# Where the next pair's projections stand in TensorE's order: key halves among the levels, three products at each place among the blocks

## The chip, the cores and the metric

The kernel runs on one core of one Trainium2 chip, in float32. The metric is the device time of one execution, in microseconds (us); the number before is the median of 3 runs.

## What is computed

The reference is one step of a two-layer decoder (RWKV-7 time mixing, then a Conformer convolution, each followed by an expert retrieval over 16384 experts). Only the time mixing is touched here. For each of the 1024 features the normed input is mixed with its neighbour token, and products with weights give receptance r, key k, value v; low-rank products give the decay w and the rate a:

```python
xm = x[None] + xx[None] * mu[:, None, None, :]
r, k, v = jnp.einsum('ibtd,ide->ibte', xm[:3], w_rkv)
w = -jax.nn.softplus(-(w0 + jnp.tanh(xw @ w1) @ w2).astype(f32)) - 0.5
a = jax.nn.sigmoid((a0 + (xa @ a1) @ a2).astype(f32))
kk = kk / jnp.maximum(jnp.sqrt(jnp.sum(kk * kk, axis=-1, keepdims=True)), 1e-12)
def step(S, inp):
    sa = jnp.einsum('bhij,bhj->bhi', S, -kk_t)
    S = (S * w_t[:, :, None, :] + sa[..., None] * (kk_t * a_t)[:, :, None, :]
         + v_t[..., None] * k_t[:, :, None, :])
    return S, jnp.einsum('bhij,bhj->bhi', S, r_t)
```

There are 512 prompt tokens and 8 x 8 sample tokens (576 columns in all), and 16 heads of 64 features.

## The kernel before

Two heads (128 features, one partition each) are a pair; there are 8 pairs, worked on one after the other by the function `wkv`. Each engine has its own hand-written instruction stream in `wkv` (blocks `pe`, `act`, `dve`, `pool`, `sp`), and engines wait for one another by counting semaphores. The class `Steps` gives each named step of an engine its count; the list of names (lines 256 to 272) must be in the order of the stream, and a name with "+" belongs to the next pair.

The scan over 512 prompt tokens is done in 4 blocks of 128. For pair i TensorE (lines 475 to 626) does, in this order:

- **bonus** (line 487) and the **grams** (lines 453 and 506): products between the factors at, bt, kt, rt of the pair, which VectorE makes last (`make_factors`, lines 838 to 848; its last instruction is the small MEMSET of line 848, and the first gram waits for it).
- **the levels** (lines 510 to 554), l = 1 to 6, which invert a triangular matrix by doubling. A level is: transposes and products "y" (lines 520, 528, 531) for two groups, a copy out of PSUM by ScalarE (line 722), a transpose to tokens in levels 1 to 3 (line 460), a place for filler, the products "dXT" (line 551), and an addition by VectorE (line 903, in the last level the copy of line 905), for which the next level's y waits.
- **the blocks** (lines 590 to 613), b = 0 to 3, a chain through the state: `rows_R` (lines 560, 563), ScalarE's copy (line 730), `rows_U` (line 572), ScalarE's copy (line 734), `rows_Y_S` (lines 577 to 585), VectorE's `update_state` (lines 913 to 920), and the next R waits for that. Between any two there is a place for filler.
- **mean** (line 617), what is left of the filler, the gate product (line 445) and **var** (line 625). VectorE centres y between mean and var (line 941), ScalarE squares it (line 772).

The filler is the generator `front(n)` with n = i + 1: the next pair's projections. `fill(count)` takes count steps of it. A step is one product of 128x128 weights with 288 columns (line 365; in the trace two matmuls, in the program's order one), or a pair of decay and rate products (lines 375, 376), or one norm sum (line 371). There are 52 steps: key half 0 (8), decay and rate (2), key half 1 (8), receptance half 0 and 1 (16), norm sums (2), value half 0 and 1 (16). By `fill` 8 are spent in the levels (0, 1, 1, 2, 2, 2), 40 among the blocks, and 4 are left behind mean. In the last pair (i = 7) there is no next front: its levels have no filler, and the blocks are filled with products of the output projection (line 469).

What VectorE does for the next pair stands in its stream between the block updates (lines 923 to 945): `logs` behind update 0, `rated_key` behind 1, `norm_floor` and two of four reciprocals behind 2, and behind update 3 the other two reciprocals, `unit_key`, `bonus_terms`, the centring of this pair's y, and `make_factors`. The core of it:

```python
update_state(3)
reciprocal(nrm, 2); reciprocal(nrm, 3)
unit_key(n)
bonus_terms(n)
dve.wait_ge(pe_s.sem, pe_s.value(f"mean.{i}"))
stt(out=in_two(yc[i]), ...)
make_factors(n)
```

ScalarE copies and squares the key (`key`, lines 643 to 650), makes the decay and rate (640, 641), the receptance (657), the key norm (661), the exponentials (674 to 679). SyncE's queue reloads the three weight buffers when k1, r1 and v1 of the pair are done (lines 335 to 340). Behind the eight pairs comes the retrieval and the convolution (lines 1000 and following), where 1152 indirect loads move most of the bytes.

Of the kernel before, what the change touches and what calls it, by code (L numbers as in the profile page):

```python
# [35 lines left out]
LEVELS = 7  # L36
# [150 lines left out]
def wkv(nc, K, I, normed, low_in, xm, y_out, hid_wa, hid_g, R, xm_at, wo_done, x_back, low2, prm, low_loaded, prm_loaded, wl):  # L187
# [8 lines left out]
    f = lambda: R.cut(N)  # L196
# [31 lines left out]
    yc, ysq = ([one] * (C - 1) + [Z.cut(T)] for one in (Q3.cut(T), Q3.cut(T)))  # L228
    sd = ysq
# [16 lines left out]
    def passes(front, steps):  # L246

        names = [f"{x}.0" for x in front.split()]
        for i in range(C):
            for x in steps:  # L250
                n = i + x.startswith("+") - x.startswith("-")
                if 0 <= n < C:
# [3 lines left out]
    pe_s = Steps(K.sem("wkv_pe"), passes("wa0 wa1 n1 n0 g",  # L256
                 ["bonus"] + [f"gram_{x}{e}" for x in ("L", "LT", "G", "RB", "RK") for e in range(2)]
                 + [x for l in range(1, LEVELS) for x in (f"y{l}_0", f"y{l}_1",
                                                         {1: "tok_v", 2: "tok_b", 3: "tok_k", LEVELS - 1: "+k0"}.get(l),
                                                         f"dXT{l}_0", f"dXT{l}_1") if x]  # L260
                 + "R0 +wa0 +wa1 U0 Y0 S0 R1 +k1 U1 Y1 S1 +r0 R2 U2 Y2 S2 +r1 +n1 +n0 R3 U3 +v0 Y3 S3 mean +v1 +g var".split()))
    act_s = Steps(K.sem("wkv_act"), passes("k0 k1 w0 a0 w1 a1 r0 r1 n1 n0 exps v0 v1 g",
                  ["gram_L0", "gram_L1"]
                  + [x for l in range(1, LEVELS) for x in (f"y{l}_0", f"y{l}_1",
                                                          {1: "tok_v", 2: "tok_b", 3: "tok_k"}.get(l)) if x]
                  + "+k0 R0 +w0 +a0 +w1 +a1 U0 R1 U1 +k1 +exps +r0 R2 U2 +r1 +n1 +n0 R3 U3 +v0 Y +v1 ysq +g sd".split()))
    dve_s = Steps(K.sem("wkv_dve"), passes("logs kf kk rk factors",
                  ["bonus"] + [f"{x}{e}" for x in ("maskLT", "level0_") for e in range(2)]
                  + [f"gram{x}{e}" for x in ("G", "RB", "RK") for e in range(2)]
# [12 lines left out]
    K_BANK, R_BANK, N_BANK, V_BANK, WA_BANK = (2, 3), (2, 3), (5, 4), (6, 7), ((4, 5), (6, 7))  # L282
# [43 lines left out]
    with nc.Block() as block:  # L326
# [35 lines left out]
        def _(pe):  # L362
            def project(n, src, j, h, name, bank):
                for k in range(C):
                    last = pe.matmul(ps[:, bank, 0:HALF], K.w[j][:, k, :], src[:, k, of_half(h)], start=k == 0, stop=k == C - 1)  # L365
                    if k == C - 1:
                        last.then_inc(pe_s.at(f"{name}{h}.{n}"), 1)
                    yield
# [51 lines left out]
            def front(n):  # L420

                pe.wait_ge(wl[0], n * 16 + 16)
                pe.wait_ge(dve_s.sem, dve_s.value(f"gramRK0.{n - 1}"))
                yield from project(n, xm[1], 0, 0, "k", K_BANK[0])
                pe.wait_ge(low_loaded, n * 16 + 16)
                for h in range(2):
                    decay_and_rate(n, h)
                    yield
                yield from project(n, xm[1], 0, 1, "k", K_BANK[1])
                pe.wait_ge(wl[1], n * 16 + 16)  # L430
                pe.wait_ge(act_s.sem, act_s.value(f"k0.{n}"))
                yield from project(n, xm[0], 1, 0, "r", R_BANK[0])
                pe.wait_ge(act_s.sem, act_s.value(f"k1.{n}"))
                yield from project(n, xm[0], 1, 1, "r", R_BANK[1])
                for h in (1, 0):
                    norm_sums(n, h)
                    yield
                pe.wait_ge(wl[2], n * 16 + 16)
                for h in range(2):
                    yield from project(n, xm[2], 2, h, "v", V_BANK[h])  # L440
# [36 lines left out]
            for i in range(C):  # L477
                ahead = front(i + 1) if i < C - 1 else output_so_far()

                def fill(count):  # L480
                    for _ in range(count):
                        next(ahead, None)
# [27 lines left out]
                for l in range(1, LEVELS):  # L510
                    corner = l == LEVELS - 1
                    for g in range(2):
                        if l > 1:
                            pe.wait_ge(dve_s.sem, dve_s.value(f"XT{l - 1}_{g}.{i}"))
                        elif g == 0:
                            pe.wait_ge(dve_s.sem, dve_s.value(f"gramG1.{i}"))
                        for b in range(2):
                            for e in range(2):
                                for j in range(1 if corner else 2):
                                    last = pe.matmul(ps[of_head(j ^ e), 4 * g + e, b * HD:(b + 1) * HD], XTd[of_head(j), e, 2 * g + b, :],  # L520
                                                     K.ident2[of_head(j)], start=True, stop=True)
                        if not corner:
                            pe.wait_ge(pool_s.sem, pool_s.value(f"co{l}_{g}.{i}"))
                        for b in range(2):
                            for e in range(2):
                                for j in range(0 if corner else 2):
                                    out = ps[of_head(j ^ e), 4 * g + e, Y_AT + b * HD // 2:Y_AT + (b + 1) * HD // 2]
                                    last = pe.matmul(packed(out, l), co[l % 2][g][of_head(j), e, b, :], later(XTd[of_head(j), e, 2 * g + b, :], l),
                                                     start=True, stop=True)
                                if corner:  # L530
                                    last = pe.matmul(ps[of_head(e), 4 * g + 1 - e, Y_AT + b * HD:Y_AT + (b + 1) * HD], L_low[HD:P, e, 2 * g + b, :],
                                                     XTd[HD:P, e, 2 * g + b, :], start=True, stop=True)
                        last.then_inc(pe_s.at(f"y{l}_{g}.{i}"), 1)
                    if l == 1:
                        pe.wait_ge(dve_s.sem, dve_s.value(f"gramRB1.{i}"))
                        tokens(i, "tok_v", v_s, 6)
                    if l == 2:
                        pe.wait_ge(dve_s.sem, dve_s.value(f"gramRK1.{i}"))
                        tokens(i, "tok_b", bt, 7)
                    if l == 3:  # L540
                        pe.wait_ge(act_s.sem, act_s.value(f"tok_v.{i}"))
                        tokens(i, "tok_k", kt, 6)
                    if i < C - 1:
                        fill((0, 0, 1, 1, 2, 2, 2)[l])
                    for g in range(2):
                        pe.wait_ge(act_s.sem, act_s.value(f"y{l}_{g}.{i}"))
                        for b in range(2):
                            for e in range(2):
                                for j in range(1 if corner else 2):
                                    q, width = of_head(j ^ e), HD if corner else HD // 2  # L550
                                    last = pe.matmul(ps[of_head(j), 4 * g + e, D_AT + b * width:D_AT + (b + 1) * width],
                                                     XY[g][q, e, b * HD:(b + 1) * HD],
                                                     XY[g][q, 1 - e if corner else e, Y_AT + b * width:Y_AT + (b + 1) * width], start=True, stop=True)
                        last.then_inc(pe_s.at(f"dXT{l}_{g}.{i}"), 1)
# [37 lines left out]
                rows_U(0)  # L592
                fill(3)
                rows_Y_S(0)
                fill(2)
                rows_R(1)
                fill(3)
                rows_U(1)
                fill(3)
                rows_Y_S(1)  # L600
                fill(4)
                rows_R(2)
                fill(3)
                rows_U(2)
                fill(3)
                rows_Y_S(2)
                fill(4)
                rows_R(3)
                fill(4)
                rows_U(3)  # L610
                fill(4)
                rows_Y_S(3)
                fill(4)
                pe.wait_ge(act_s.sem, act_s.value(f"Y.{i}"))
                pe.wait_ge(dve_s.sem, dve_s.value(f"state{NB - 1}.{i}"))
                for h in range(2):
# [19 lines left out]
        def _(act):  # L636
# [6 lines left out]
            def key(n, h):  # L643
                if n:
                    act.wait_ge(pe_s.sem, pe_s.value(f"k{h}.{n}"))
                else:
                    act.wait_ge(mix_pe.sem, mix_pe.value("key"))
                got = ps[:, K_BANK[h] if n else 4 + h, 0:HALF]
                act.activation(k_s[:, of_half(h)], got, ACT.Copy)
                act.activation(sq[:, of_half(h)], got, ACT.Square, scale=prm[:, K_K:K_K + 1]).then_inc(act_s.at(f"k{h}.{n}"), 1)  # L650
# [61 lines left out]
            for i in range(C):  # L712
# [15 lines left out]
                def rows_R(b):  # L728
                    act.wait_ge(pe_s.sem, pe_s.value(f"R{b}.{i}"))
                    act.activation(r_tok, ps[:, 0, 0:P], ACT.Copy).then_inc(act_s.at(f"R{b}.{i}"), 1)  # L730
# [5 lines left out]
                if more:  # L736
                    act.wait_ge(prm_loaded, n * 16 + 16)
                    key(n, 0)
                rows_R(0)
                if more:  # L740
                    decay_and_rate(n, 0)
# [2 lines left out]
                rows_R(1)  # L744
                rows_U(1)
                if more:
                    key(n, 1)
                    for part in range(3):
                        exps(n, part)
                    receptance(n, 0)  # L750
# [1615 lines left out]
```

## Time and profile before

| | |
|---|---|
| median of 3 runs | 3720.38 us (3717.39 to 3723.23) |
| profiled execution, its own time | 3720.96 us |
| its span | 3719.2 us |
| PE / DVE / ACT / POOL busy | 2813.9 / 2674.9 / 1453.8 / 1433.9 us |
| the eight pairs | about 86 to 578 us of the span |
| weight products of line 365 (7 pairs) | 672 matmuls, 189.5 us |

A busy time counts executed instructions only. Matmuls overlap by their pipeline, so the time that one takes of the engine is the distance between two starts, not its own duration. A row's "idle before" is the time in which the engine had nothing to run, with the instruction of the other engine that ended it. The clock column is TensorE's granted clock as a share of 2.4 GHz; 0.50 is 1.2 GHz.

### The profile page before, as it was taken

The numbers are of one execution on the slowest core, as the hardware profiler recorded it, in microseconds if no ns is written. First come the engines' busy times: TensorE is split into PE (matmuls) and PEld (weight loads), VectorE is DVE, ScalarE is ACT, GpSimd is POOL, SyncE is SP. The second block draws the span as 40 slices with busy tenths as digits, with TensorE's granted clock in tenths as the row PEclk, the third lists the DMA queues.
The fourth block names the chain that finished last, engine by engine and source line by source line (L and its number), as shares of the span: only waits on it lengthen the run. The fifth ranks groups of instructions, "written<-read, shape, count | busy, mean of one in ns | idle before, by whom it ended". The sixth has DMA issues, their size and how long they took to land.

```text
span 3719.2 us, 56236 instructions
## 1 busy us (share of the span) xinstructions
PE 2813.9 (76%) x20324; PEld 1333.2 (36%) x20324; DVE 2674.9 (72%) x6281; ACT 1453.8 (39%) x4371; POOL 1433.9 (39%) x1305
## 2 busy tenths in 40 slices
PE   7999996777787578787787768887886666666655
PEld 4777774323332124343332223443331222222111
DVE  7454644888676677877877778998676777777775
ACT  3434432333343344444444334444443333333333
POOL 0111111444444444434444444334454444444442
PEclk9999997888897779988798779999896877887878
DMA  2010114999999999999999999999999999999997
GB/s 91 21 40 21 40 47 161 425 426 425 426 426 427 426 427 416 382 414 421 411 420 427 427 426 425 400 374 384 396 419 426 426 426 427 426 427 426 427 426 311
DMA packets 198279, 1312.95 MB, mean 353 GB/s; under 512 B 25968, under 2 KB 34288, under 8 KB 44272
## 3 DMA queue, kind: packets, MB, share of 16 engines
q0 software_dynamic: 165888, 1208.03, 77.6%
q1 hardware_dynamic: 32112, 101.33, 7.0%
q8 instruction: 159, 2.61, 0.3%
q14 instruction: 120, 0.98, 0.1%
HBM read 1303.42 MB, written 5.86 MB: 352 GB/s over the span
## 4 chain that ended last, share of the span: by engine, by line
DMA 34%; DVE 21%; PE 19%; ACT 4%; issue 3%; DVEq 2%; POOL 1%; ACTq 1%; SPq 0%; POOLq 0%
DMA arena<-in_uv,arena 34%; DVE arena L1922 10%; PE psum L1334 8%; PE psum L1296 4%; PE psum L1494 3%; PE psum L1524 2%; DVE arena L2111 2%; ACT wbuf L1665 1%; DVE arena L1850 1%; ACT arena L1660 1%; POOL arena L1276 1%; DVE arena L2085 1%; DVE arena L1847 1%; DVE arena L1854 1%; ACT arena L1656 1%
## 5 line engine op out<-in xcount | busy, mean ns | idle before, releaser
L1334 PE MATMUL psum<-arena,wbuf 64*64 64x512 f32 (+1 forms) x8704 | 1455.5, 739 | 803.4 <-ACT wbuf L1665 797.5
L1276 POOL DMA_INDIRECT arena<-in_uv,arena x1152 | 1359.4, 1180 | 1737.6 <-PE psum L1334 1559.4
L1922 DVE SCALAR_TENSOR_TENSOR arena<-arena 128x1024 f32<-128x1024 f32 x1152 | 1392.3, 1222 | 480.5 <-DMA arena<-in_uv,arena 453.1
L1334 PEld LDWEIGHTS psum<-arena,wbuf 64*64 64x64 f32 (+1 forms) x8704 | 335.1, 153 | 1674.4 <-ACT wbuf L1665 1304.2
L1656 ACT ACTIVATE arena<-arena 128x2 f32<-128x2 f32 x576 | 117.0, 203 | 1663.3 <-DVE arena L1922 1644.0
L1665 ACT ACTIVATE wbuf<-cst,arena 128x64 f32<-128x64 f32 x1152 | 338.2, 340 | 40.8 <-issue 1.4
L1296 PE MATMUL psum<-arena,wbuf 128*128 128x256 f32 (+1 forms) x1024 | 311.8, 453 | 9.7 <-DVE arena L1933 5.8
L1660 ACT ACTIVATE arena<-arena 128x1 f32<-128x1 f32 x1152 | 276.7, 287 | 41.8 <-issue 2.4
L1296 PEld LDWEIGHTS psum<-arena,wbuf 128*128 128x128 f32 x1024 | 202.8, 208 | 170.5 <-issue 129.2
L365 PE MATMUL psum<-arena,wbuf 128*128 128x288 f32 x672 | 189.5, 414 | 0.0
L2111 DVE SCALAR_TENSOR_TENSOR arena<-arena,par 128x256 f32<-128x256 f32 x240 | 115.7, 482 | 48.3 <-ACT arena L1763 42.6
L1656 ACT ACT_TABLE_LOAD x107 | 137.3, 1283 | 19.3 <-DVE arena L1922 17.0
L1514 PE MATMUL psum<-arena 128*128 128x256 f32 (+1 forms) x512 | 137.0, 415 | 0.0
L962 POOL COPY arena<-arena 64x256 f32<-64x256 f32 x8 | 3.2, 397 | 331.6 <-DVE x L848 331.6
L365 PEld LDWEIGHTS psum<-arena,wbuf 128*128 128x128 f32 x672 | 117.9, 190 | 26.8 <-issue 2.7
L1494 PE MATMUL psum<-arena 128*128 128x320 f32 (+1 forms) x384 | 113.2, 439 | 16.7 <-ACT arena L1775 16.3
L1524 PE MATMUL psum<-arena 64*64 64x256 f32 x1024 | 123.3, 392 | 0.0
L1514 PEld LDWEIGHTS psum<-arena 128*128 128x128 f32 x512 | 93.6, 190 | 57.9 <-issue 36.8
L913 DVE SCALAR_TENSOR_TENSOR x<-psum,arena,cst 128x128 f32<-128x128 f32 x32 | 11.2, 350 | 138.4 <-PE psum L585 138.4
L1646 ACT ACT_TABLE_LOAD x79 | 101.4, 1283 | 4.9 <-issue 1.0
L1494 PEld LDWEIGHTS psum<-arena 128*128 128x128 f32 x384 | 72.0, 196 | 71.2 <-issue 34.7
L1922 DVE DVE_READ_ACCUMULATOR arena<-arena 128x1 f32 x1152 | 94.7, 82 | 0.0
(311 smaller groups left out, 3121.7 us busy)
## 6 DMA issues: line engine op xcount, KB each, us to landing
wbuf<-in_w_q SPq DMA_DIRECT2D x32, 1152.0 KB
arena<-in_uv,arena POOLq DMA_INDIRECT x1152
arena<-in_w_pw SPq DMA_DIRECT2D x16, 1024.0 KB
wbuf<-in_w_rkv SPq DMA_DIRECT2D x24, 512.0 KB, 4.4
arena<-in_w_o SPq DMA_DIRECT2D x16, 512.0 KB, 7.3
arena<-in_w_pw SPq DMA_DIRECT2D x16, 512.0 KB
x<-in_x SPq DMA_DIRECT2D x4, 576.0 KB, 7.3
arena<-in_state SPq DMA_DIRECT2D x8, 256.0 KB
```

Source lines behind the costliest of these rows:

```text
L365: last = pe.matmul(ps[:, bank, 0:HALF], K.w[j][:, k, :], src[:, k, of_half(h)], start=k == 0, stop=k == C - 1)
L1276: pool.indirect_dma_start(ring[:, g % RING, :], None, I["uv"][p // 2], bass.IndirectOffsetOnAxis(ap=idx[:, s % 4, j:j + 1], axis=0)).then_ ...
L1296: last = pe.matmul(ps[:, 7, 0:WIDTH[half]], K.w9[j][:, k, :], h[half][:, k, :], start=k == 0, stop=k == C - 1)
L1334: last = pe.matmul(ps[e * HD:(e + 1) * HD, 2 * (u % 2) + a if u < NB else 4, :], diag[t, g % DIAGS, :], ring[t, g % RING, D + e * 512:D + ...
L1494: last = pe.matmul(ps[:, BANK[c % 2], 0:WIDTH[half]], weights[c % 2][:, k, :], src[:, k, :], start=k == 0, stop=k == C - 1)
L1514: last = pe.matmul(out, wb[j][:, k, :], h[half][:, k, :], start=k == 0, stop=k == C - 1)
L1524: last = pe.matmul(part[q], tap_diags[q, k, :], ups[c % 2][q, k:k + 2 * P], start=k == 0, stop=k == PE_TAPS - 1)
L1656: act.activation(gelu[:, q], dots[:, q], ACT.Gelu)
L1660: act.activation(coef[:, c:c + 1], gelu[:, c:c + 1], ACT.Copy, scale=share[:, s % 4, j + k:j + k + 1])
L1665: act.activation(diag[:, (g + k) % DIAGS, :], K.ident2, ACT.Copy, scale=coef[:, c:c + 1]).then_inc(diag_ready, 1)
L1922: stt(out=row, in0=row, scalar=1.0, in1=tok[p % 2][:, UNITS[p % 2].index(u), :], op0=ALU.mult, op1=ALU.mult, accum_out=dots[:, g % COLS:g ...
L2111: last = stt(out=out, in0=up[:, k:k + 2 * P], scalar=K.par[:, TAP0 + k, c:c + 1], in1=out, op0=ALU.mult, op1=ALU.add)
```

## The change

The steps of `front` stand in another order: both key halves first, then decay and rate. The fills in levels 1 to 6 become 0, 2, 2, 4, 4, 4 (16 steps, before 8), and each of the 12 places from R0 to behind S3 takes 3 steps (36; before 40, of 2, 3 and 4), so that none is left behind mean. ScalarE takes key half 1 before its R0 copy, not behind U1, and TensorE waits for the rate of half 1 (`a1`) before the norm sums, which the wait for `k1` did before. The numbers of steps and the work are the same.

```diff
-                                                         {1: "tok_v", 2: "tok_b", 3: "tok_k", LEVELS - 1: "+k0"}.get(l),
+                                                         {1: "tok_v", 2: "tok_b", 3: "tok_k", LEVELS - 3: "+k0", LEVELS - 1: "+k1"}.get(l),
-                 + "R0 +wa0 +wa1 U0 Y0 S0 R1 +k1 U1 Y1 S1 +r0 R2 U2 Y2 S2 +r1 +n1 +n0 R3 U3 +v0 Y3 S3 mean +v1 +g var".split()))
+                 + "R0 +wa0 +wa1 U0 Y0 S0 R1 +r0 U1 Y1 S1 +r1 R2 +n1 +n0 U2 Y2 S2 R3 +v0 U3 Y3 S3 +v1 mean +g var".split()))
...
                 yield from project(n, xm[1], 0, 0, "k", K_BANK[0])
+                yield from project(n, xm[1], 0, 1, "k", K_BANK[1])
                 pe.wait_ge(low_loaded, n * 16 + 16)
                 for h in range(2):
                     decay_and_rate(n, h)
                     yield
-                yield from project(n, xm[1], 0, 1, "k", K_BANK[1])
...
                 yield from project(n, xm[0], 1, 1, "r", R_BANK[1])
+                pe.wait_ge(act_s.sem, act_s.value(f"a1.{n}"))
                 for h in (1, 0):
                     norm_sums(n, h)
...
-                        fill((0, 0, 1, 1, 2, 2, 2)[l])
+                        fill((0, 0, 2, 2, 4, 4, 4)[l])
...
                 rows_Y_S(0)
-                fill(2)
+                fill(3)
                 rows_R(1)
                 fill(3)
                 rows_U(1)
                 fill(3)
                 rows_Y_S(1)
-                fill(4)
+                fill(3)
                 rows_R(2)
                 fill(3)
                 rows_U(2)
                 fill(3)
                 rows_Y_S(2)
-                fill(4)
+                fill(3)
                 rows_R(3)
-                fill(4)
+                fill(3)
                 rows_U(3)
-                fill(4)
+                fill(3)
                 rows_Y_S(3)
-                fill(4)
+                fill(3)
...
                     key(n, 0)
+                    key(n, 1)
                 rows_R(0)
...
-                    key(n, 1)
                     for part in range(3):
                         exps(n, part)
```

How TensorE's order moves, at two places (line numbers behind line 425 are one higher in the changed kernel). The first is levels 4 and 5 of pair 0, before:

```order
L520 MATMUL psum<-cst,arena 64x64 x8
L528 MATMUL psum<-arena 64x32 x8
L365 MATMUL psum<-arena,wbuf 128x288 x2
L551 MATMUL psum<-arena 64x32 x16
L520 MATMUL psum<-cst,arena 64x64 x8
L528 MATMUL psum<-arena 64x32 x8
L520 MATMUL psum<-cst,arena 64x64 x8
L528 MATMUL psum<-arena 64x32 x8
L365 MATMUL psum<-arena,wbuf 128x288 x2
L551 MATMUL psum<-arena 64x32 x16
```

and with the change:

```order
L521 MATMUL psum<-cst,arena 64x64 x8
L529 MATMUL psum<-arena 64x32 x8
L365 MATMUL psum<-arena,wbuf 128x288 x4
L552 MATMUL psum<-arena 64x32 x16
L521 MATMUL psum<-cst,arena 64x64 x8
L529 MATMUL psum<-arena 64x32 x8
L521 MATMUL psum<-cst,arena 64x64 x8
L529 MATMUL psum<-arena 64x32 x8
L365 MATMUL psum<-arena,wbuf 128x288 x4
L552 MATMUL psum<-arena 64x32 x16
```

Four weight products instead of two stand between y and dXT of each of these levels.

The second place is the seam from S3 of pair 0 (line 585) to the grams of pair 1, before:

```order
L585 MATMUL psum<-arena 128x128
L365 MATMUL psum<-arena,wbuf 128x288 x4
L617 MATMUL psum<-x,cst 128x256 x2
L365 MATMUL psum<-arena,wbuf 128x288 x4
L445 MATMUL psum<-arena 128x288 x2
L625 MATMUL psum<-x,cst 128x256 x2
L487 MATMUL psum<-arena,cst 128x288 x2
L453 MATMUL psum<-arena 64x64 x40
```

and with the change:

```order
L586 MATMUL psum<-arena 128x128
L365 MATMUL psum<-arena,wbuf 128x288 x3
L618 MATMUL psum<-x,cst 128x256 x2
L446 MATMUL psum<-arena 128x288 x2
L626 MATMUL psum<-x,cst 128x256 x2
L488 MATMUL psum<-arena,cst 128x288 x2
L454 MATMUL psum<-arena 64x64 x40
```

One product ahead of mean and all four behind it have gone from here.

## Rows read from the trace of the kernel before

**Rows 1.** Windows: start:end, us, busy of each engine, clock, DMA share, GB/s.
```profile
207.90:268.60 60.70, 57.31 (x890) 45.70 (x890) 33.23 (x69) 24.98 (x52) 9.10 (x19) 1.00 0.09 32
```

**Rows 2.** VectorE's last instruction of make_factors: duration, first and last start.
```profile
L848 DVE MEMSET x<- x8: 165/165/165, 85.3 to 509.6; 128x128 f32 x8
```

**Rows 3.** Waits from 86 to 510 us: sum, times, longest.
```profile
DVE arena L827 <- ACT arena L661: 15.7, 7, 2.3
...
PE psum L453 <- DVE x L848: 7.0, 7, 1.0
...
PE psum L560 <- DVE arena L905: 4.9, 7, 0.7
...
PE psum L560 <- DVE x L920: 2.2, 7, 0.6
```

**Rows 4.** PE's timeline, level 4 of pair 2: start, us, what, [idle before].
```profile
222.15 1.24 PE L365 MATMUL psum<-arena,wbuf 128*128 128x288 f32 x4
223.32 0.67 PE L551 MATMUL psum<-arena 64*64 64x32 f32 x32
224.16 0.46 PE L520 MATMUL psum<-cst,arena 64*64 64x64 f32 x16 [0.18 <-DVE arena L903]
```

**Rows 5.** ACT's timeline: level 4's two copies, then the square before var.
```profile
221.80 0.96 ACT L722 ACTIVATE arena<-psum 128x384 f32<-128x384 f32 x2 [1.37 <-PE psum L528]
...
264.80 0.62 ACT L772 ACTIVATE x<-x 128x512 f32<-128x512 f32 x1
```

**Rows 6.** PE's timeline, filler before R1 and before R2 of pair 2.
```profile
236.38 1.14 PE L365 MATMUL psum<-arena,wbuf 128*128 128x288 f32 x4
238.14 0.49 PE L560 MATMUL psum<-x,arena 128*128 128x128 f32 x2 [0.62 <-DVE x L920]
...
243.72 2.11 PE L365 MATMUL psum<-arena,wbuf 128*128 128x288 f32 x8
245.67 0.38 PE L560 MATMUL psum<-x,arena 128*128 128x128 f32 x2
```

**Rows 7.** DVE's timeline: the last step of update 1.
```profile
244.78 0.29 DVE L920 TENSOR_SCALAR x<-arena 128x128 f32<-128x128 f32 x1
```

**Rows 8.** PE's timeline, the seam from S3 of pair 2 to pair 3.
```profile
259.32 0.39 PE L585 MATMUL psum<-arena 128*128 128x128 f32 x2
...
261.49 1.03 PE L617 MATMUL psum<-x,cst 128*128 128x256 f32 x4
262.35 2.11 PE L365 MATMUL psum<-arena,wbuf 128*128 128x288 f32 x8
264.30 1.14 PE L445 MATMUL psum<-arena 128*128 128x288 f32 x4
265.48 1.13 PE L625 MATMUL psum<-x,cst 128*128 128x256 f32 x4
266.44 1.14 PE L487 MATMUL psum<-arena,cst 128*128 128x288 f32 x4
268.59 0.58 PE L453 MATMUL psum<-arena 64*64 64x64 f32 x22 [1.01 <-DVE x L848]
```

**Rows 9.** DVE's timeline, the same seam.
```profile
259.75 0.35 DVE L913 SCALAR_TENSOR_TENSOR x<-psum,arena,cst 128x128 f32<-128x128 f32 x1 [2.46 <-PE psum L585]
...
260.44 1.96 DVE L823 RECIPROCAL arena<-arena 128x144 f32<-128x144 f32 x2
...
263.94 0.68 DVE L941 SCALAR_TENSOR_TENSOR x<-psum,x 128x512 f32<-128x512 f32 x1
...
268.37 0.17 DVE L848 MEMSET x<- 128x128 f32 x1
```

**Rows 10.** Windows, PE alone: start:end, us, PE busy, granted clock, DMA share, GB/s.
```profile
508.00:510.00 2.00, 1.00 (x12) 1.00 0.94 358
...
518.00:520.00 2.00, 0.70 (x32) 1.00 0.13 47
520.00:522.00 2.00, 1.82 (x64) 0.87 0.04 8
522.00:524.00 2.00, 2.00 (x48) 0.50 0.00 0
...
584.00:586.00 2.00, 0.28 (x2) 1.00 0.36 55
586.00:588.00 2.00, 0.00 (x0) 0.58 0.82 336
```

More of the change, by code:

```diff
@@ L265, in wkv @@
                                                           {1: "tok_v", 2: "tok_b", 3: "tok_k"}.get(l)) if x]
-                  + "+k0 R0 +w0 +a0 +w1 +a1 U0 R1 U1 +k1 +exps +r0 R2 U2 +r1 +n1 +n0 R3 U3 +v0 Y +v1 ysq +g sd".split()))
+                  + "+k0 +k1 R0 +w0 +a0 +w1 +a1 U0 R1 U1 +exps +r0 R2 U2 +r1 +n1 +n0 R3 U3 +v0 Y +v1 ysq +g sd".split()))
     dve_s = Steps(K.sem("wkv_dve"), passes("logs kf kk rk factors",
```

## The prediction

> **What bounds the kernel now.** I read the page first: over the whole span DMA and VectorE lead the chain that ended last, but that is the retrieval behind the pairs. It starts from the pairs' output, so what the pairs take is added to the end one for one, and only they are changed. Second, the windows: over one pair TensorE is busy 57.31 of 60.70 us, VectorE 33.23, ScalarE 24.98, at full clock [rows 1]. The eight factor memsets lie from 85.3 to 509.6 us, so a pair is (509.6 - 85.3) / 7 = 60.6 us [rows 2]. TensorE's stream is the bound, and its idle time is all that a new order of the same work can win. Third, the waits show where that is: 1.0 us a pair at the seam, for the factors; 0.7 us before R0; 0.3 us a pair before R1 (2.2 us over 7) [rows 3]; and 0.18 us at each of five levels [rows 4]. The other places where one engine hands to another are covered by filler.
>
> **The price of a product.** Before R2 eight matmuls, four products, start at 243.72 and R2 starts at 245.67 [rows 6]: 1.95 / 4 = 0.49 us each. The change moves such products and adds none.
>
> **1. Eight more products in the levels (+3.9 us a pair).** Filler there covers ScalarE's two copies out of PSUM. In level 4 they start at 221.80 and end 0.96 later, at 222.76 [rows 5]; the two products run from 222.15, and dXT starts at 223.32 [rows 4], 0.56 us after the second copy. So two products already cover the copies, and two more stand in the open. In levels 2 and 3 the tokens' transposes and one product stand there already. The level's own wait, 0.18 us before the next y [rows 4], lies behind dXT, where no filler stands, and stays; so does the 0.7 us before R0 [rows 3]. Sum: 8 x 0.49 = +3.9 us. Bounds: all eight in the open, +3.9; two or so hidden in unseen slack, +3.0. I take 3.9.
>
> **2. Four of them come out from among the blocks, ahead of S3 (-1.8 us a pair).** Before R1 there is one more product (2 to 3): it costs 0.49 and fills the 0.3 us of wait, so +0.2. Before R2 and R3 there is one less (4 to 3). Update 1 ends at 244.78 + 0.29 = 245.07 [rows 7], and three products from 243.72 end at 245.18 [rows 6]: three just cover the update, so each place gives its whole 0.49. If the update were late there as it is before R1, up to 0.3 of each would come back as a wait. The places behind R3 and U3 (4 to 3 each) must cover a ScalarE copy, which three products do behind R1, U1, R2 and U2 with no wait on TensorE in the list; 0.49 each. Sum: 0.2 - 4 x 0.49 = -1.8; bounds -2.0 and -1.2.
>
> **3. Five come out of the seam, behind S3 (0 us).** This is the step that decides. From S3 on VectorE works without a gap worth naming: update 3 at 259.75, reciprocals at 260.44, the centring at 263.94, the memset that frees the grams until 268.37 + 0.17 = 268.54, and the grams start at 268.59 [rows 8, 9]. That is 8.8 us of VectorE from S3, in an order that the change doesn't touch; TensorE's 4 + 4 products lie beside it. With one product less ahead of mean and none behind it, mean runs from about 261.0 (it was 261.49), and the centring at 263.94 is not waiting for it either way. The gate product follows and ends near 263.0. Var has to wait for ScalarE's square, 264.80 + 0.62 = 265.42 [rows 5], and starts at 265.48 as before; bonus follows at 266.44, the grams at 268.59 [rows 8]. So 5 x 0.49 = 2.4 us of work go, and a new wait of 2.4 us before var takes their place. What the earlier norm sums bring does not help here: the wait that they shorten (15.7 us over 7 pairs, VectorE on the key norm) [rows 3] lies before update 3, where VectorE then waits for S3 anyway, 2.46 us [rows 9]. Gain 0; bounds 0 and -0.2.
>
> **4. ScalarE and the queues (0).** Key half 1 (two activations of 0.4 to 0.5 us) now stands before the R0 copy. Key half 0 no longer arrives there late, R0 waits for VectorE's last copy in any case, and ScalarE has time between. If it were late, `U0` and all of the chain behind it would wait; I put at most +0.3 a pair. Weight reloads are released earlier or at the same time. The new wait for `a1` stands many us behind the rate. In the last pair the output products, smaller than 0.49 each, spread differently: 0, with -2 to +2.
>
> **5. The clock at the seam (+3 in all, bounds 0 and +14).** Today the seam leaves TensorE idle for 1.0 us and the clock stays at 2.4 GHz, as in the stretch 508 to 510 [rows 8, 10]. It does not after longer pauses: after 518 to 520 with 0.70 of 2 us busy it fell to 1.2 GHz, and after 584 to 586 with 0.28 busy too [rows 10]. The new seam holds 2.4 us idle, then 1.95 us of var and bonus, then 1.0 us idle: more idle than today's and less than behind 584, so I expect a fall at some of the seven seams. What one costs: var and bonus take 3.9 instead of 1.95 us and end at 269.4, 0.8 us behind the memset; a fall that comes later slows the first grams instead, some 2 us at most. Four seams at 0.8 make 3. The Trainium skill, "TensorE: Matmul & The Clock Gate", section "HAM oscillation — how this bites in real kernels", describes this: waits between bursts of matmuls bring the clock back to half. [...]
>
> **Sum.** Steps 1 to 4: 3.9 - 1.8 + 0 + 0 = +2.1 us a pair, x 7 pairs with a next front = +15; step 5: +3. The sum is made against the profiled execution, 3720.96 us (span 3719.2), which lies 0.6 over the median: 3739, against the median 3738. By the bounds of the steps: 7 x (3.0 - 2.0 - 0.2) = +6 and 7 x (3.9 - 1.2 + 0.3) + 14 = +35; neither end has all its parts at once, so the likeliest case's own range is 3730 to 3750.
>
> **The rivals.**
> *The clock stays low into the levels.* In pair 7, whose levels have no filler, the clock stays at 0.50 from 522 us on [rows 10]. If the seam's fall outlasts the grams (4.5 us at full clock, so +4) and level 1 (+2), a seam costs 6, and four seams 24: 15 + 24 = +39, 3759. Against it: the grams are dense work, and the levels hold more filler now, which speaks for a rise.
> *The levels hide the products (not slower).* If TensorE's time in levels 4 to 6 were set by the chain y, copy, dXT, addition, and not by its own stream, six of the eight products would be free: 7 x (3.9 - 2.9 - 1.8) = -6, 3715. It turns the sign from the point where five of eight are hidden. Against it is the 0.56 us between the copy's end and dXT [rows 4, 5], and that the only wait left stands behind dXT.
> *The seam was TensorE's and not VectorE's.* Were the memset pulled ahead by what TensorE sheds, 7 x 2.4 = 17 would come back: 15 - 17 = -2, 3719, no difference. For it speaks that TensorE waits only 1.0 us there; against it VectorE's unbroken rows [rows 9].
> *The change does nothing measurable,* because a slip elsewhere (a stalled fetch of instructions, a late reload) covers it: 3722.
>
> **How the numbers follow.** No change can be told within 0.2%, 7.4 us, that is 3713 to 3728. The forecast, 3738: 0.75. The clock low into the levels, 3759: 0.09. Levels hide the products: 0.05, a third of it faster by over 0.2%. The seam was TensorE's: 0.06. Nothing measurable: 0.05. So faster 0.02, same 0.13, slower 0.85. The range, 3727 to 3751, takes in the forecast's own range and a part of the cases on either side.
>
> **What would show it.** Right: line 365 unchanged in count (672 matmuls) and busy time; a level 4 that is 0.97 us longer; TensorE idle for about 2.4 us before var (line 626 then) with ScalarE's square as releaser, and still 1.0 before the grams; 8.8 us from S3 to the memset; the memsets 62.7 us apart; the key norm's wait of VectorE gone and its wait for S3 longer; stretches of clock below 1.00 at some seams. Wrong: pairs 60 to 61 us apart, or the memset less than 8.5 us behind S3 (step 3), or levels 4 to 6 of unchanged length (step 1), or new waits before R1 to R3 (step 2).

## The result, and the profile after

| | before | with the change |
|---|---|---|
| median of 7 runs each | 3722.53 us | 3733.18 us (3731.77 to 3734.87) |
| ratio, 95% interval | | 1.0033 (1.0023 to 1.0042) |
| profiled execution, its span | 3720.96, 3719.2 us | 3733.08, 3731.3 us |
| eight memsets of `make_factors`, start to start | 60.6 us | 62.9 us |

The changed kernel is slower by 10.65 us, 12.1 us between the two profiled executions; 3738 was forecast, within 3727 to 3751. The change's own line numbers are one higher behind line 425.

VectorE's last instruction of `make_factors` answers to [rows 2]; (526.7 - 86.4) / 7 = 62.9 us a pair:

```profile
L849 DVE MEMSET x<- x8: 165/165/165, 86.4 to 526.7; 128x128 f32 x8
```

The waits from 86 to 525 us (sum, times, longest) answer to [rows 3]:

```profile
PE psum L626 <- ACT x L773: 16.3, 7, 2.3
...
PE psum L561 <- DVE arena L906: 4.9, 7, 0.7
...
PE psum L454 <- DVE x L849: 3.8, 4, 1.1
```

The first is new: TensorE waits 2.3 us before var at all seven seams. The wait before R0 is as it was, the one before R1 (VectorE's line 921 now) has gone from TensorE's list.

TensorE's timeline of pair 2: level 4, then the filler before R2. It answers to [rows 4, 6].

```profile
228.88 2.21 PE L365 MATMUL psum<-arena,wbuf 128*128 128x288 f32 x8
231.02 0.67 PE L552 MATMUL psum<-arena 64*64 64x32 f32 x32
231.86 0.46 PE L521 MATMUL psum<-cst,arena 64*64 64x64 f32 x16 [0.18 <-DVE arena L904]
...
253.37 1.62 PE L365 MATMUL psum<-arena,wbuf 128*128 128x288 f32 x6
254.83 0.42 PE L561 MATMUL psum<-x,arena 128*128 128x128 f32 x2
```

The filler of level 4 takes 231.02 - 228.88 = 2.14 us instead of 1.17, so its two added products cost 0.97, and the level's own wait of 0.18 us is still there. Before R2 three products take 1.46 us (254.83 - 253.37) and R2 starts with no wait: they just cover the update.

The seam of pair 2 on TensorE, then on VectorE and ScalarE, answers to [rows 5, 8, 9]:

```profile
267.11 0.39 PE L586 MATMUL psum<-arena 128*128 128x128 f32 x2
267.33 1.62 PE L365 MATMUL psum<-arena,wbuf 128*128 128x288 f32 x6
268.79 1.02 PE L618 MATMUL psum<-x,cst 128*128 128x256 f32 x4
269.65 1.14 PE L446 MATMUL psum<-arena 128*128 128x288 f32 x4
273.13 1.57 PE L626 MATMUL psum<-x,cst 128*128 128x256 f32 x4 [2.33 <-ACT x L773]
274.50 2.13 PE L488 MATMUL psum<-arena,cst 128*128 128x288 f32 x4
276.55 1.85 PE L454 MATMUL psum<-arena 64*64 64x64 f32 x80
```

```profile
267.53 0.35 DVE L914 SCALAR_TENSOR_TENSOR x<-psum,arena,cst 128x128 f32<-128x128 f32 x1 [3.43 <-PE psum L586]
...
271.73 0.68 DVE L942 SCALAR_TENSOR_TENSOR x<-psum,x 128x512 f32<-128x512 f32 x1
...
276.15 0.17 DVE L849 MEMSET x<- 128x128 f32 x1
```

```profile
272.44 0.63 ACT L773 ACTIVATE x<-x 128x512 f32<-128x512 f32 x1 [3.04 <-DVE x L942]
```

From update 3 to the memset VectorE takes 276.15 - 267.53 = 8.62 us; before it took 268.37 - 259.75 = 8.62 us [rows 9]. TensorE has shed five products and stands still instead. At this seam bonus takes 2.05 us to the next start, not 1.07, since the clock fell. Granted clock (the last but two) in windows of 1 us there:

```profile
273.00:274.00 1.00, 0.87 (x3) 0.84 1.03 369
...
275.00:276.00 1.00, 1.00 (x4) 0.50 0.76 269
...
277.00:278.00 1.00, 1.00 (x66) 0.96 0.00 0
```

It fell like that at three of the seven seams.

Read off VectorE's starts (memset, and line 913, now 914, for S0 to S3), the typical pair is this; the first two columns are of the trace before and after, the others of experiments told below:

| us | before | change | before_levels8 | blocks_to_seam | after_tail4 |
|---|---|---|---|---|---|
| memset to S0 | 28.88 | 32.77 | 32.77 | 28.96 | 32.37 |
| S0 to S3 | 22.81 | 20.96 | 22.81 | 20.96 | 19.50 |
| S3 to memset | 8.62 | 8.62 | 8.62 | 8.62 | 8.62 |
| mean of 7 pairs | 60.6 | 62.9 | 64.5 | 59.0 | 60.8 |

The typical pair leaves out what pairs 0 to 2 have besides (0.4 to 1.3 us each, with and without the change); that stands in the means. The change has its three falls of the clock in pairs 1, 3 and 6 on top.

### The profile page after: what moved, and what is told of

It is laid out like the page before. It is cut to its first block, busy times and chain, and to the rows that moved or that the text cites. A ratio compares the mean times of both kernels' runs of the same rounds, so it can differ in the third digit from the quotient of the medians.

```text
span 3731.3 us, 56236 instructions
## 1 busy us (share of the span) xinstructions
PE 2802.5 (75%) x20324; PEld 1329.4 (36%) x20324; DVE 2674.1 (72%) x6281; ACT 1451.8 (39%) x4371; POOL 1428.0 (38%) x1305
## 4 chain that ended last, share of the span: by engine, by line
DMA 35%; DVE 21%; PE 18%; ACT 4%; issue 3%; DVEq 2%; POOL 1%; ACTq 1%; SPq 0%; POOLq 0%
DMA arena<-in_uv,arena 34%; DVE arena L1923 10%; PE psum L1335 8%; PE psum L1297 4%; PE psum L1495 3%; DVE arena L2112 2%; PE psum L1525 2%; ACT wbuf L1666 1%; POOL arena L1277 1%; ACT arena L1661 1%; DVE arena L1851 1%; DVE arena L2086 1%; DVE arena L1848 1%; DVE arena L1855 1%; ACT arena L1657 1%
## 5 line engine op out<-in xcount | busy, mean ns | idle before, releaser
L1515 PEld LDWEIGHTS psum<-arena 128*128 128x128 f32 x512 | 93.6, 190 | 58.1 <-issue 36.9
```

The lines of the kernel that those rows point to most:

```text
L1515: last = pe.matmul(out, wb[j][:, k, :], h[half][:, k, :], start=k == 0, stop=k == C - 1)
```

## The experiments

The theory: the seam from S3 to the memset is set by VectorE's 8.62 us, so products put there are free up to TensorE's wait, and every product elsewhere costs its 0.49 us. The rivals: TensorE's own work sets the seam too (every product costs the same anywhere); or the levels hide a part of their filler.

**after_seam4: four useless products in the new wait.** Their result is not used.

```diff
 gate_terms(i + 1)
+for k in range(4):
+    pe.matmul(ps[:, 2, 0:HALF], K.headones, hid_g[:, 0:HALF], start=True, stop=True)
```

> The changed kernel with four more products (the gate hidden values against a constant, 288 columns, result unused) behind the gate product of each of the seven pairs that have a next one, ahead of var. If VectorE's chain of 8.6 us from S3 to the factor memset sets the seam, they stand in the 2.3 us of wait before var: memsets stay 62.9 us apart, time 3733 us, 3731 to 3735, and the clock doesn't fall at the seams any more. If TensorE's own work sets it, each costs 0.49 us: 7 x 1.95 = 13.6 more, 3747 us.

Measured: 3733.51 us, ratio 1.0028 (1.0015 to 1.0040), where the change itself has 1.0033. The memsets lie 62.7 us apart. The seam of pair 2 on TensorE:

```profile
270.16 2.10 PE L625 MATMUL psum<-arena,cst 128*128 128x288 f32 x8
272.65 1.13 PE L628 MATMUL psum<-x,cst 128*128 128x256 f32 x4 [0.39 <-ACT x L775]
273.62 1.14 PE L488 MATMUL psum<-arena,cst 128*128 128x288 f32 x4
275.90 1.63 PE L454 MATMUL psum<-arena 64*64 64x64 f32 x80 [1.15 <-DVE x L851]
```

The wait before var is 0.39 instead of 2.33 us: 1.95 us of products went in and moved nothing. The clock doesn't fall at any seam here, and with that the pairs behind a fall are 0.4 to 0.6 us shorter: memset to S0 is 32.77 in pairs 3 and 6, where it was 33.17 and 33.20 with the change, and 34.04 instead of 34.63 in pair 1. 62.9 - 62.7 = 0.2 us a pair, 1.4 us in all, is the price of the falls by these two profiles; the medians are too rough for it.

**before_seam4: the same four in the kernel before.** The same edit behind `gate_terms(i + 1)`.

> The kernel before with the same four added products behind the gate product of each of seven pairs. If the seam is VectorE's chain with TensorE 1.0 us short of it, the first two are free and the others are in the open: 7 x (1.95 - 1.01) = 6.6 more than before, 3729 us. If every product on TensorE costs its 0.49 us: 13.6 more, 3736 us.

Measured: 3722.69 us, ratio 1.0005 (0.9996 to 1.0015). The memsets lie 61.1 us apart, 0.5 a pair more, where 0.94 was expected. The seam:

```profile
266.45 1.14 PE L445 MATMUL psum<-arena 128*128 128x288 f32 x4
267.43 2.10 PE L624 MATMUL psum<-arena,cst 128*128 128x288 f32 x8
269.37 1.02 PE L627 MATMUL psum<-x,cst 128*128 128x256 f32 x4
270.23 1.14 PE L487 MATMUL psum<-arena,cst 128*128 128x288 f32 x4
271.30 1.63 PE L453 MATMUL psum<-arena 64*64 64x64 f32 x80
```

Now TensorE goes through without a wait, and start-to-start distances give the true room. Gate to the next start is 0.98 us, var to bonus 0.86, bonus to grams 1.07. Before they were 1.18, 0.96 and 2.15 [rows 8]. So the seam had 0.20 + 0.10 + 1.08 = 1.38 us of room, not the 1.01 of the idle column: two short waits before var and bonus didn't show as idle time, since the modelled end of a matmul (0.40 us behind its start) overlapped them. 1.95 - 1.38 = 0.57, and memset to S0 grew from 28.88 to 29.43. The theory holds, its room was mis-sized, and with it the 3729 us that were expected.

**before_levels8: eight useless products in the levels.** Two behind the filler of each of levels 3 to 6; the result is not used.

```diff
 fill((0, 0, 1, 1, 2, 2, 2)[l])
+for k in range(2 if l > 2 else 0):
+    pe.matmul(ps[:, 3, 0:HALF], K.headones, hid_g[:, 0:HALF], start=True, stop=True)
```

> The kernel before with two added products (result unused) behind the filler of each of levels 3 to 6 of seven pairs. If filler there stands in the open: 7 x 8 x 0.49 = 27 more, 3750 us, and S0 comes 3.9 us later behind the memset. If the chain of y, copy, dXT and addition covers a part of it, as the rival said, less: 3736 us or under if half is covered.

Measured: 3749.39 us, ratio 1.0073 (1.0056 to 1.0090). In level 5 of pair 2 the two added ones and dXT behind them:

```profile
236.53 1.24 PE L365 MATMUL psum<-arena,wbuf 128*128 128x288 f32 x4
237.61 1.13 PE L546 MATMUL psum<-arena,cst 128*128 128x288 f32 x4
238.67 0.67 PE L553 MATMUL psum<-arena 64*64 64x32 f32 x32
```

Memset to S0 is 32.77, the same 3.89 us as with the change. The levels hide none of eight products; that rival is gone.

**after_tail4: one step of the change undone, with real work.** Two products instead of three behind each of R0 to R3, and four left behind mean again; the levels stay as changed.

```diff
 rows_R(0)
-fill(3)
+fill(2)
```

and the same behind `rows_R(1)`, `rows_R(2)` and `rows_R(3)`, with the names of TensorE's steps in the new order.

> The changed kernel with one product less at each of the four places behind R0 to R3 (2 instead of 3) and these four products left behind mean again, where the kernel before has them. The work is the same. If they stand for nothing at the seam (VectorE's chain), each of the four saves its 0.49 us among the blocks: S0 to S3 shorter by 1.5 (three of the places lie there), S3 to memset 8.62 as ever, memset to S0 32.8 less 0.5, memsets 60.9 us apart, 7 x 1.95 = 13.6 under the changed kernel: 3720 us, which is the kernel before within 2. If the seam is TensorE's, 3733 us as with the change; if two products behind R don't cover ScalarE's copy, between the two.

Measured: 3720.60 us, ratio 1.0001 (0.9992 to 1.0010), and 60.8 us a pair. The four products stand in the seam of pair 2:

```profile
262.87 2.10 PE L365 MATMUL psum<-arena,wbuf 128*128 128x288 f32 x8
264.81 1.14 PE L446 MATMUL psum<-arena 128*128 128x288 f32 x4
266.34 1.13 PE L626 MATMUL psum<-x,cst 128*128 128x256 f32 x4 [0.39 <-ACT x L773]
...
269.59 1.63 PE L454 MATMUL psum<-arena 64*64 64x64 f32 x80 [1.15 <-DVE x L849]
```

They are free there, and they save what they cost where they stood: S0 to S3 is 19.50 instead of 20.96 us, 1.46 for three, and memset to S0 0.40 less for the fourth. So the change's eight products in the levels (+3.9) are paid back, all but 0.2 us, by eight from the blocks (-1.85 ahead of S3 by the change, and 1.46 + 0.40 = 1.86 a pair more here). What the change lost, it lost by emptying the seam. Two products behind R cover ScalarE's copy nearly as well as three: what was saved there is within 0.1 us of the full 0.49 each.

**blocks_to_seam: the products from the blocks into the seam.** The levels as before, three products at each place, eight behind mean. For this the norm sums go ahead of receptance half 1, and ScalarE takes receptance half 1 behind U3, value half 0 behind Y. The first of these lines stands behind S0, the second behind S1, S2, R3, U3 and S3.

```diff
-fill(2)
+fill(3)
...
-fill(4)
+fill(3)
```

> The kernel before with the levels' filler as it was (8), three products at each of the twelve places among the blocks, and the eight that are left behind mean; the norm sums stand before receptance half 1, and ScalarE takes receptance half 1 behind U3 and value half 0 behind Y. The half of the change that takes products from the blocks, without the half that puts them into the levels. From S0 to S3 1.9 us less, at the seam TensorE's work grows by 3 products to 0.4 us over VectorE's chain: 7 x (0.4 - 1.9) = -10, 3712 us. If the seam had been TensorE's own: 7 x (3 x 0.49 - 1.9) = -3, 3720 us. If a copy of ScalarE comes late by its new order: slower than 3722.

Measured: 3711.11 us, ratio 0.9963 (0.9949 to 0.9978). The seam of pair 2:

```profile
258.37 1.02 PE L617 MATMUL psum<-x,cst 128*128 128x256 f32 x4
259.23 4.05 PE L365 MATMUL psum<-arena,wbuf 128*128 128x288 f32 x16
263.12 1.14 PE L445 MATMUL psum<-arena 128*128 128x288 f32 x4
264.09 1.03 PE L625 MATMUL psum<-x,cst 128*128 128x256 f32 x4
264.95 1.14 PE L487 MATMUL psum<-arena,cst 128*128 128x288 f32 x4
266.02 1.63 PE L453 MATMUL psum<-arena 64*64 64x64 f32 x80
```

TensorE has no wait left there. The three products more in the seam cost 0.08 us (memset to S0, 28.88 to 28.96), which is 3 x 0.49 less the room of 1.38 found by before_seam4. S0 to S3 is 1.85 us shorter, and a pair takes 59.0 us.

**hole_at_R0: one more hole.** As blocks_to_seam, with one of level 6's two products behind dXT, in the wait before R0.

```diff
-fill((0, 0, 1, 1, 2, 2, 2)[l])
+fill((0, 0, 1, 1, 2, 2, 1)[l])
...
+if i < C - 1:
+    fill(1)
 pe.wait_ge(dve_s.sem, dve_s.value(f"XT{LEVELS - 1}_1.{i}"))
```

> As blocks_to_seam, and one of level 6's two products stands behind dXT instead of ahead of it, in the 0.7 us in which TensorE waits for VectorE's copy before R0. If that wait is a hole: memset to S0 0.3 to 0.5 us less, 7 x 0.4 = 3 under blocks_to_seam, 3708 us. If the product delays R0 because ScalarE's key copy comes behind it, or dXT waits for ScalarE's copy: 3711 us or more.

Measured: 3710.08 us, ratio 0.9964 (0.9950 to 0.9977). The pairs are 0.4 us shorter, as expected: memset to S0 28.42 in the shortest, memsets (496.3 - 86.0) / 7 = 58.6 us apart. The whole is not measurably faster than blocks_to_seam: 3 us were expected, and the intervals are about 5 us to either side. The last pair took 36.90 us from memset to S0 in this profiled execution (30.59 in that one), more than the seven pairs won. What happens there was the next question.

**before_last8 and hole_and_last8: filler in the last pair's levels.** Eight useless products in levels 2 to 6 of pair 7 alone.

```diff
+else:
+    for k in range((0, 0, 1, 1, 2, 2, 2)[l]):
+        pe.matmul(ps[:, 3, 0:HALF], K.headones, hid_g[:, 0:HALF], start=True, stop=True)
```

> The kernel before with eight added products (result unused) in levels 2 to 6 of the last pair alone, as the other pairs have there. If the last pair's sparse levels are what lets the clock fall, it stays at 2.4 GHz there, and memset to S0 of pair 7 is 28.9 us like the others' instead of 32.4: 3.5 us less, 3718 us. If the fall and the 1.5 us stall come from something else (the load of the output weights), the products add up to 3.9: 3725 us.

> hole_at_R0 and before_last8 together. By the theory 3.0 to 3.5 us under hole_at_R0 if its last pair loses the clock as before, less if it falls late there as in the changed kernel (29.4): 3705 to 3708 us. By the rival 3709 to 3712.

Measured: 3721.14 us, ratio 0.9999 (0.9990 to 1.0008), and 3709.83 us, ratio 0.9968 (0.9958 to 0.9979); neither can be told from the kernel it was made from. In before_last8 the clock is low for 3.4 us instead of 17, and memset to S0 of pair 7 is 31.20 against 32.43 before, where 28.9 was expected. The 1.2 us are a balance: the clock and a pause shorter by 0.3 us give back more than the eight products cost (3.9 us at full clock); the runs don't part these. In hole_and_last8 it is 36.6. TensorE's waits from 495 to 534 us in that kernel:

```profile
PE psum L520 <- issue: 3.8, 2, 2.7
```

It stands still for 3.8 us with no semaphore that the profile shows to wait for, while the output weights' loads run or just behind them; in the kernel before it was 1.5 us, with the change 0.6 and 0.4. (The last section has what the traces say of these pauses.) Dense levels alone don't make the last pair short.

**before_paced, hole_paced, hole_paced_last8: the loads one by one.** The theory was that eight loads of 512 KB issued together hold up what TensorE waits for.

```diff
 for c in range(C):
+    if c >= 2:
+        sp.wait_ge(pe_s.sem, pe_s.value(("gram_L1", "y1_1", "y2_1", "y3_1", "y4_1", "y5_1")[c - 2] + f".{i}"))
     sp.dma_start(wo[:, c * C:(c + 1) * C, :], I["w_o"][c]).then_inc(wo_loaded, 16)
```

> The kernel before, where SyncE starts the third to eighth of the eight loads of the output weights (512 KB each) one by one, behind the last pair's gram L and behind y of levels 1 to 5, instead of all at once. If TensorE's 1.5 us pause in the last pair comes from these loads, it goes or shrinks under 0.5 us, memset to S0 of pair 7 falls from 32.4 to about 30, less if the clock falls later too: 1.5 to 4 us less, 3718 us. If the pause has another cause: as before, 3721 us.

> hole_at_R0 with the paced loads. Its last pair took 36.9 us from memset to S0, with 2.1 us of pause and 28 us of half clock. If the loads are the cause: 29 to 31 us there, 3703 us. If not: 3710 us.

> hole_and_last8 with the paced loads. It had 3.8 us of pause and 36.6 us from memset to S0 in the last pair. If the loads are the cause and the added products keep the clock: 28.5 us there, 3702 us. If not: 3710 us.

Measured: 3718.68 us, ratio 0.9995 (0.9986 to 1.0004); 3702.95 us, ratio 0.9954 (0.9940 to 0.9967); 3703.81 us, ratio 0.9960 (0.9946 to 0.9973). TensorE's waits of this kind in the last pair, for before_paced and then for hole_paced:

```profile
PE psum L533 <- issue: 1.3, 1, 1.3
...
PE psum L530 <- issue: 0.5, 1, 0.5
```

```profile
PE psum L553 <- issue: 1.3, 1, 1.3
```

So the pause isn't removed: 1.8 us against 1.5 in the kernel before, and 1.3 against 2.1 in hole_at_R0. Memset to S0 of the last pair is 30.61 and 30.12 us, as expected if the loads were the cause, but the pause that was to go is still there, and with the loads as they were this stretch took anything from 29.4 to 36.9 us. Only in hole_paced_last8 there is none, and there the last pair takes 28.74 us from memset to S0 at full clock (fields: us, busy of each engine, clock 1.00):

```profile
495.90:524.70 28.80, 26.98 (x724) 22.34 (x723) 15.43 (x35) 9.85 (x22) 9.13 (x18) 1.00 0.41 135
```

The theory on the loads is not shown by one such profile. The medians of the last two are the lowest of the study, 17 us under the kernel before and 30 under the changed one, but their intervals overlap those of hole_at_R0 and blocks_to_seam; that pacing the loads helps is not shown either.

## Why the prediction was right, and where its sizes were off

**Step 1, the levels: right.** +3.9 was forecast, memset to S0 grew from 28.88 to 32.77, +3.89, and before_levels8 gives the same 3.89 with other products.

**Step 2, the blocks: right.** -1.8 was forecast, S0 to S3 went from 22.81 to 20.96, -1.85. No new wait before R1 to R3, and three products cover the update as worked out.

**Step 3, the seam: right, and it decides.** VectorE's 8.62 us from S3 to the memset is the same in every kernel of the study, with from 3 to 12 products of filler beside it. The five products that left became the wait of 2.33 us before var (forecast 2.4). after_seam4 shows that four put back cost nothing, after_tail4 that leaving real ones there gives the whole loss back. The key norm came early, as said, and VectorE waits for S3 longer, 3.43 against 2.46 us. What was mis-sized is the room before the change: 1.38 us and not 1.01 (before_seam4). It doesn't enter the sum.

**Steps 1 to 3 together.** +2.04 a pair, 14.3 us over seven. The memsets' distance from first to last grew from 424.3 to 440.3, 16.0 us; the seams' clock and a scatter of 0.3 us are the rest.

**Step 5, the clock: mechanism right, size off.** Forecast four falls at 0.8 us, 3 in all, with a bound of 14. There were three at 0.4 to 0.6, 1.4 in all by after_seam4. A fall costs less than worked out because its first half lies in the room beside VectorE: at the seam shown bonus takes 1 us longer, of which 0.2 reach the grams. The rival with the clock low into the levels didn't come: the clock is back within 4 us, during the grams. The Trainium skill, "TensorE: Matmul & The Clock Gate", section "HAM oscillation — how this bites in real kernels", shows such falls behind waits of 3 to 5 us between bursts of matmuls. No wait of a seam is longer than 2.3 us here, so that example says nothing for a fall at every seam; the trace has one at three of seven.

**Step 4, the last pair: the term that failed.** It was put at 0, between -2 and +2. From its memset to the start of the last output products it took 578.29 - 509.63 = 68.66 us before and 592.36 - 526.74 = 65.62 with the change, -3.0. Ten profiled executions of kernels whose last pair has no filler in its levels, the two of before and change among them, have memset to S0 at 29.4 to 36.9 us, so the 3.0 is within what this pair does by itself: it all lies there, 32.43 against 29.42. What the change does to this pair is seen behind S0, and comes to nothing. S0 to S3 is 21.31 us in every kernel with the fills of before and 19.99 with three at each place, 1.32 less, and from S3 to the last output products (line 631, now 632) it is 14.92 and 16.21 us, 1.29 more: the output products only moved. Two windows from the memset to S0, before and with the change (the third from the end is the clock):

```profile
509.60:542.10 32.50, 29.17 (x706) 25.84 (x707) 15.55 (x36) 9.97 (x21) 9.19 (x18) 0.74 0.27 102
```

```profile
526.70:556.20 29.50, 26.01 (x706) 22.50 (x707) 15.42 (x36) 9.92 (x21) 9.14 (x18) 0.88 0.21 82
```

**The sum.** Between the profiled executions: +1.1 before the first memset, where nothing was changed, +16.0 in seven pairs, -3.0 in the last, -2.0 in the retrieval: +12.1. The forecast had 15 + 3 = 18 and took the rest for unchanged. The -2.0 is no work of the change that can be seen: from the last output products to the end the 13 profiled kernels, whose instructions are the same there, take from 3138.0 to 3144.2 us (3140.9 before, 3138.9 with the change). So what the pairs take reaches the end one for one only within some 3 us. The two differences lie within what unchanged code scatters, and that both went down, 5 us together, is luck of this pair of profiles. The seven pairs alone give 16.0 where 18 was forecast, so the steps hold better than the total of 12.1 looks.

**The rivals.** "The levels hide the products" fell by before_levels8, "the seam was TensorE's" by after_seam4, "nothing measurable" by the interval of the result. The stalled fetch that the last one named may be real, but shows in the last pair alone in both traces (see the last section).

## What to carry to other kernels

Filler has a place where another engine is longer: before it is moved, measure that engine's chain from the point that starts it to the point that ends the stretch, and compare start-to-start distances, not the idle column. A busy share of 94% (57.31 of 60.70 us) says that a new order can win little, not that it can't lose: here the same 52 steps took 62.9, 60.6 or 58.6 us a pair by their places alone. The best order filled the seam to VectorE's length, took products from the blocks, and put one product into the wait before R0: 3703 to 3711 us in the five kernels with the first two (four of them with the third), against 3720 to 3721 before.

## What the runs showed that was not expected

The idle time of TensorE's column was too small by 0.37 us at one seam: 0.20 and 0.10 us of waiting were covered by the modelled ends of matmuls.

The last pair, with no filler in its levels, is a source of scatter: low clock for 7 to 27 us and pauses of TensorE of 1.0 to 2.2 us in sum, at other instructions in each kernel (3.8 us in one with filler). Neither dense levels nor paced loads alone removed the pauses; both together had none in the one profile taken.

The pauses bear a mark of the fetching of instructions. The one of the kernel before, and the instruction queue's share of the DMA from 516 to 521 us (packets, MB, share):

```profile
519.30 0.40 PE L520 MATMUL psum<-cst,arena 64*64 64x64 f32 x12 [1.52 <-issue]
```

```profile
q8 instruction: 2, 0.03, 2.9%
```

The first of these two packets, of 16384 bytes, starts at 517.0 us and takes 1.1 us; TensorE goes on at 519.30, 2.3 us behind its start. So it is everywhere. The last pair has 25 such pauses in the twelve kernels that have any, and each ends 2.2 to 2.7 us behind the start of a packet of that queue, no two of which start closer together than 3.3 us there. And counted over all of TensorE's weight loads and matmuls, the places of the pauses are whole multiples of 256 instructions apart, within one instruction. TensorE then waits for its next instructions, by all that the traces show; no run was made for it, and why the packet comes too late in one kernel and not in another stays open, the output weights' loads among the possible causes.

The low clock goes with the pauses. In each of the twelve kernels it first falls between 0.1 us before and 3.2 us after the end of one. In hole_paced_last8, which has none, it doesn't fall before 559 us, behind the levels and the blocks.
